# One 8 KB run per partition for the experts' output weights, and transposes that take every other column

## The reference, cut to what matters

```python
for e in range(N_EXPERTS):                      # 32
    z = hf @ w_moe_in[e] + b_moe_in[e]          # (256, 1024) @ (1024, 2048)
    zg = jnp.minimum(z[:, ::2], SWIGLU_LIMIT)
    zl = jnp.clip(z[:, 1::2], -SWIGLU_LIMIT, SWIGLU_LIMIT)
    act = zg * jax.nn.sigmoid(SWIGLU_ALPHA * zg) * (zl + 1.0)
    out = out + gates[:, e:e + 1] * (act @ w_moe_out[e] + b_moe_out[e])   # (.., 1024) @ (1024, 1024)
```

## Time and profile before

| what | value |
|---|---|
| time, median of 3 runs | 1265.28 us (1265.22 to 1267.68) |
| span of the profiled execution, first to last instruction | 1265.8 us |
| PE busy | 1199.6 us, 95% of the span |
| DVE, ACT, POOL busy | 375.0, 161.6, 93.7 us |
| HBM read | 433.52 MB |
| busy share of the DMA queue that SP feeds | 84.7% of 16 engines' span |
| mean granted clock of the matrix engine | 0.980 |

### The profile page before, as it was taken

The page is one execution under the profiler, slowest core; times in us unless marked ns, Lnnn a source line. Parts: engine busy times, 40 slices in busy tenths (PEclk is TensorE's granted clock), DMA queues, the critical chain, the costliest instruction groups (busy, mean ns, idle before and its releaser), DMA issues.

```text
span 1265.8 us, 14071 instructions
## 1 busy us (share of the span) xinstructions
PE 1199.6 (95%) x5406; PEld 544.6 (43%) x5406; DVE 375.0 (30%) x750; ACT 161.6 (13%) x307; POOL 93.7 (7%) x70
## 2 busy tenths in 40 slices
PE   7786959998999999999999999999999999999996
PEld 6775737886333333333333333333333333333332
DVE  4979957213111122121111111112212111111112
ACT  4000143403000000010000000000010000000002
POOL 4745610000000000000000000000000000000000
PEclk9987979999999999999999999999999999999999
DMA  7522342378999986999999999999999999999993
GB/s 221 164 67 67 111 189 100 128 306 311 392 422 418 422 337 273 421 421 420 421 419 422 418 422 417 423 418 423 419 422 419 422 420 421 421 420 421 419 420 149
DMA packets 105468, 434.98 MB, mean 344 GB/s; under 512 B 13528, under 2 KB 36384, under 8 KB 72672
## 3 DMA queue, kind: packets, MB, share of 16 engines
q1 hardware_dynamic: 104864, 433.47, 84.7%
q10 hardware_dynamic: 576, 1.13, 0.2%
HBM read 433.52 MB, written 1.05 MB: 343 GB/s over the span
## 4 chain that ended last, share of the span: by engine, by line
PE 87%; DVE 7%; ACT 2%; issue 2%; POOL 1%; DMA 0%; DVEq 0%; ACTq 0%; POOLq 0%
PE ps L1450 35%; PE ps L1492 18%; PE ps L1425 9%; PE ps L1409 5%; PE ps L1459 4%; PE ps L1176 4%; DVE ring L755 3%; PE ps L1229 3%; PE ps L1360 2%; DVE ring L884 2%; PE ps L1476 1%; PE ps L1417 1%; PE ps L1350 1%; DVE late L917 1%; PE ps L1209 1%
## 5 line engine op out<-in xcount | busy, mean ns | idle before, releaser
L1450 PE MATMUL ps<-ring,late 128*64 128x512 f32 x1024 | 225.2, 592 | 0.2 <-issue 0.2
L1083 DVE TENSOR_SCALAR late<-ps 128x512 f32<-128x512 f32 x32 | 22.1, 691 | 661.8 <-PE ps L1450 661.8
L1492 PE MATMUL ps<-ring,late 128*64 128x512 f32 x896 | 198.5, 594 | 0.0
L1450 PEld LDWEIGHTS ps<-ring,late 128*64 128x64 f32 x1024 | 74.3, 137 | 145.1 <-issue 145.1
L1425 PE MATMUL ps<-late 128*128 128x512 f32 x256 | 118.4, 605 | 0.8 <-ACT late L725 0.8
L1450 PE MATMUL ps<-wbuf,late 128*64 128x512 f32 x512 | 115.8, 593 | 0.0
L1492 PEld LDWEIGHTS ps<-ring,late 128*64 128x64 f32 x896 | 62.9, 137 | 121.5 <-issue 118.9
L718 ACT ACTIVATE late<-late 128x512 f32<-128x512 f32 x32 | 20.1, 630 | 504.4 <-DVE late L1083 504.4
L1425 PEld LDWEIGHTS ps<-late 128*128 128x128 f32 x256 | 46.0, 189 | 72.7 <-issue 72.7
L1176 PE MATMUL ps<-x_t,wbuf 128*128 128x256 f32 x320 | 72.4, 387 | 2.7 <-ACT ring L673 1.7
L1450 PEld LDWEIGHTS ps<-wbuf,late 128*64 128x64 f32 x512 | 36.5, 137 | 73.7 <-issue 73.7
(11 more groups left out here) (210 smaller groups left out, 997.8 us busy)
## 6 DMA issues: line engine op xcount, KB each, us to landing
ring<-in_w_moe_in SPq DMA_DIRECT2D x128, 1024.0 KB, 18.5
ring<-in_w_moe_out SPq DMA_DIRECT2D x112, 1024.0 KB, 12.9
wbuf<-in_w_moe_in SPq DMA_DIRECT2D x64, 1024.0 KB, 16.9
late<-in_w_moe_in SPq DMA_DIRECT2D x16, 1024.0 KB, 21.1
mixed<-in_w_moe_in SPq DMA_DIRECT2D x16, 1024.0 KB, 22.6
x_t<-in_w_moe_in SPq DMA_DIRECT2D x16, 1024.0 KB, 23.1
late<-in_w_moe_out SPq DMA_DIRECT2D x16, 1024.0 KB, 25.7
x<-in_w_moe_in SPq DMA_DIRECT2D x16, 1024.0 KB, 24.4
```

The source lines that it names most:

```text
L1083: ve.tensor_scalar(gate_z, z[:, 0], LIMIT, None, ALU.min).then_inc(z_gate, 1)
L1450: i = pe.matmul(ps[r, n // 2, :], h_sel[:, k % 4, k // 4, :], w[:, 512 * n:512 * n + 512], start=(k == 0), stop=(k == KD - 1))
L1492: i = pe.matmul(ps[64 * q:64 * q + SLOTS, 2, :], act_tile(k), w[:, 512 * q:512 * q + 512], start=(k == 0), stop=(k == KF - 1))
```

## The change

It has two parts that belong together. In the source of chunks 8 to 11 the 256 rows are given to the partitions in another order: before, partition p took rows p and p + 128 of the chunk, two pieces of 4 KB that lie 512 KB apart; now it takes rows 2p and 2p + 1, which are one piece of 8 KB. Step k of the y product therefore needs the features of even or odd number within a group of 256, and so the four transposes of `act` take every other column (a step of 2 float32 values, 8 bytes) in place of 128 neighbouring columns. The number of bytes, transfers, matrix instructions, waits and places stays what it was, and `act_tile` and line 1492 are not touched.

```diff
@@ -207,6 +207,7 @@
         h_tok, gate_z, lin_z, sig = [cut(512 * n, 512) for n in range(4)]
         act = lin_z
+        act_rows = act.rearrange("p (b c i) -> p b i c", b=2, i=2)
@@ -337,7 +338,7 @@
             r = (c - NW_IN) * 2 * P
-            return io["w_moe_out"][bass.ds(e, 1), r:r + 2 * P, :].rearrange("o (k p) n -> p (o k) n", p=P)
+            return io["w_moe_out"][bass.ds(e, 1), r:r + 2 * P, :].rearrange("o (p k) n -> p (o k) n", p=P)
@@ -1473,7 +1474,7 @@
                     pe.wait_ge(act_ok, j + 1)
                     for n in range(4):
-                        i = pe.transpose(ps[:, 0, n * P:n * P + P], act[:, n * P:n * P + P], ident)
+                        i = pe.transpose(ps[:, 0, n * P:n * P + P], act_rows[:, n // 2, n % 2, :], ident)
                     i.then_inc(act_trans, 1)
```

## The result

The changed kernel takes 1269.93 us (median of 20 runs, the lowest 1267.16), the kernel before 1267.20 us (20 runs, 1265.22 to 1269.10). The ratio is 1.0019, 95% interval 1.0012 to 1.0026: slower by 0.19%, just inside the 0.2% that the prediction called no change, but clear of zero and outside the range of the predicted time. Three executions far above the rest of their kernels are left out of the ratios: this one's of 2542.1 us, and further down 7141.6 us with the step of four and 1799.3 us with the vector engine's reordering.

A forecast was written before the change was run, and what follows sets the result against it. The matrix engine was taken to bound the experts, with transfers hidden. Transfers, DMA disturbance and transposes summed to 0 + 0 + 0 on the profiled 1265.8 us, or 1265.3 us against the median; range about 1263.5 to 1269 us.

The forecast's parts named there:

- What bounds the kernel: Expert loop: the matrix engine sets a constant 29.32 us per expert; transfers are hidden behind it, with 6.7 us reserve.
- The transfers: Chunks 8 to 11 of `w_moe_out`: 8 KB pieces take 0.43 us less per expert, all hidden, so 0.
- Rival B: Chunks 8 to 11: transfers still cut by row into 4 KB pieces, landings unchanged, 1265.3 us; chance 0.09.
- D: Chunks 8 to 11: new transfers slower than old; at 380 GB/s 12.7 us later, 1278 us; chance 0.02.
- The transposes: Line 1476, act's four transposes: on the path; stepped loads cost 0 to 13.4 us in all, taken as 0.
- rival C: Line 1476, before the copy of line 722: stepped load slower by up to 13.4 us, to 1278.7 us; chance 0.09.
- What the y product waits for: After line 1476: longer transposes delay the scalar engine's copy and the y product's start by as much, all 32 times.
- The level: Whole run: no change from the median of the runs shown, 1265.3 us; the profiled execution's 1265.8 stands 0.5 above.

The follow-up runs named there:

- the shared copy: Kernel before, with the copy of act's plain transposes split between vector and scalar engine: 1266.90 us against 1266.98, ratio 1.0003.

## Why the prediction was right or wrong

**What bounds the kernel: right.** The transfers don't, and the halves of the change show it directly: the 8 KB loads alone left the period at 29.32 us. The period is constant in every kernel here. But a constant period wasn't proof of a fixed list of the matrix engine alone: in the changed kernel it is as constant, with a wait on the scalar engine in every expert.

**The transfers: right in sign and in what they are worth, a little off in size.** The landings were to be at 14 us or less in the last stretch: 12.0 in the changed kernel, 14.3 with the loads alone. The rate was to go towards 427 GB/s and reached 425. The backlog was to grow by 0.08 us for each expert; in the changed kernel the landings went from 8.5 to 12.0 us over the same 15.8 experts, 0.22 each. At 425 GB/s 12.583 MB take 29.6 us, so the 428 GB/s of one 16 us stretch was a little high as a mean. Rival B is out by the count of packets, and so is D: the loads alone are not slower.

**The transposes: this step failed.** The prediction gave both bounds, 0 and 13.4 us, and took 0, because a step of 8 bytes is the smallest there is. It measured 0.080 us for each expert, 2.4 us over the 30 periods of the profile and some 2.5 us in all; the transposes alone made the kernel 0.17% slower (0.08 to 0.26), which is 2.2 us. This was rival C, at a fifth of its upper bound and right at the point from which it was to decide (20 ns per load; 0.080/4 = 20). The upper bound held and was loose: it doubled the pace of all four, as if no load were hidden. The load itself grew by half (140 to 209 ns), midway between nothing and doubling; of that, 0.056 us came through at the first, and some 0.01 us at each of those that ran under the transpose ahead of them.

The Trainium skill, "Advanced Engine Details and Errata", section "Memory Cachelines", had given 0 for this step, and a penalty for a step of four. The first isn't what the matrix engine's weight loads show: 209 ns at step 2 against 140 without. A step of four does pay, but at 212 ns no more than a step of two, and a step of eight pays less, 190. The measurement decides; as a reason for taking 0 the rule was no better than the guess.

**What the y product waits for: right.** The prediction said that whatever the transposes take longer, the copy ends later and the y product starts later. So it was: the copy ends 0.09 us later, the y product starts 0.08 later, and its idle time on the copy grew by 2.3 of the loop's 2.4 us. What it didn't see is the second path. It took line 1417 as already run out, but with the 0.17 us behind its loads that line is through 0.01 us after the copy's path. The expectation for those transposes took the idle time for slack behind the copy, and that for the shared copy took it for a loss; with two paths that end together it was neither.

**The level: low by 1.9 us.** The forecast of no change was set on the median of three runs, 1265.28 us; over 20 runs the kernel before has 1267.20, and the three had two of the lowest values of all. So the miss of 1269.93 - 1265.3 = 4.6 us is 1.9 us of sampling and 2.7 us of change. Against 1267.2 the forecast would have had the result inside a range of the same width. The place of the scatter is the first part: expert 1's z group starts anywhere from 338.98 to 342.03 us in the profiles here.

No version beat the kernel before by more than the measurement can tell.

## What to carry to other kernels

When an engine works through a fixed list, the period is constant. A wait that is the same each time leaves it constant too, so look at the idle time in front of each kind of work. Then price every instruction on the list in tens of nanoseconds, since 20 ns by 128 is 0.2%, and don't let "the smallest step" stand for "free". Put a reordering where an engine has time: the vector engine took the same permutation at no cost. A wait that is put down to another engine may be worth nothing, because a second path ends at the same time; the test is to end that other work sooner. But such a test holds only for the kernel that it is made in: ending the copy sooner gained nothing with plain transposes, and with stepped ones the copy is what the y product waits for.

## What the runs showed of the hardware

- A stationary operand of 128x128 float32 read with a step loads in 209 ns (step 2), 212 (step 4) or 190 (step 8), against 140 without. That the longest step is the cheapest was not expected, and stays open.
- Of that, a group of four transposes shows 0.089 us at its end and 0.080 in the period: 0.056 us from the first load, which nothing hides, and some 0.01 from each of the others.
- Transfers of 8 KB pieces ran at 425 to 428 GB/s, 4 KB pieces at 410, in the same queue.
- The vector engine read float32 from PSUM with a step of 16 bytes as fast as with 8: 0.69 us for 128x512.
- From transposes to products with 64 columns of weights the matrix engine's load idled 0.17 us although the copy that it needed had ended 0.27 us before. Behind stepped transposes it idled 0.12 us.
- After a copy by the scalar engine, the matrix engine's load that waited for it started 0.05 us after the copy's end.
